# Second norm in plain channel order with five row buffers, square sums first, one sigmoid, and modulation blocks in pairs

## The reference, cut to what matters

```python
sh1, sc1, g1, sh2, sc2, g2 = split(silu(c) @ w_ada + b_ada)      # modulation, 6 x 1024 per row of c
h  = rmsnorm(x, norm1_g) * (1 + sc1) + sh1
q, k, v, u, gate_b, gate_c = split(h @ w_in)
x  = x + g1 * (concat(attention(q, k, v), short_conv(u, ...)) @ w_o)
h2 = rmsnorm(x, norm2_g) * (1 + sc2) + sh2                       # the second norm
scores = sigmoid(h2 @ w_router)                                  # 64 experts, top 8 of 4 groups
routed = sum over 8 chosen experts of gate * (silu(h2 @ w_gate_e) * (h2 @ w_up_e)) @ w_down_e
x  = x + g2 * (routed + shared_expert(h2))
```

## Time and profile before

| | |
|---|---|
| median of 3 runs | 1159.12 us (1158.35 to 1160.63) |
| profiled execution | 1158.43 us, span 1156.4 us |
| PE busy | 1055.1 us (91% of the span) |
| DVE / ACT / POOL busy | 431.3 / 198.2 / 183.5 us |
| mean granted TensorE clock | 0.966 of 2.4 GHz |
| DMA | 372.10 MB, 322 GB/s over the span |
| stages (us from the start) | projection to 263, attention to 370, output projection to 430, second norm and router to 457, routing to 499, expert loop to about 1090, tail |

### The profile page before, as it was taken

One profiled execution on the slowest core, in us unless ns is written; L12 is line 12 of the kernel. 1 busy time (PEld: TensorE's weight loads), 2 busy tenths in 40 slices (PEclk: granted clock), 3 DMA queues, 4 the chain that ended last, 5 costly groups with the idle time before them and its releaser, 6 DMA issues.

```text
span 1156.4 us, 15518 instructions
## 1 busy us (share of the span) xinstructions
PE 1055.1 (91%) x5570; PEld 531.4 (46%) x5570; DVE 431.3 (37%) x933; ACT 198.2 (17%) x427; POOL 183.5 (16%) x240
## 2 busy tenths in 40 slices
PE   5999899998999986889998889988899898999885
PEld 3355455676777566643342323433334333334332
DVE  0445876415554357622322212222122212222156
ACT  4311110003333013001111111111111111111100
POOL 1002223102302001321211111111011211111100
PEclk9999999998999998999998989999999988999998
DMA  9879789964663922599999999999999999999496
GB/s 306 305 276 348 255 311 322 279 218 181 219 171 117 365 78 91 215 406 359 419 404 421 378 377 417 410 408 415 381 408 410 407 355 422 387 417 380 180 411 240
DMA packets 81055, 372.10 MB, mean 322 GB/s; under 512 B 12513, under 2 KB 27438, under 8 KB 52807
## 3 DMA queue, kind: packets, MB, share of 16 engines
q1 hardware_dynamic: 50160, 269.80, 59.3%
q0 software_dynamic: 23312, 69.67, 17.4%
q10 hardware_dynamic: 7540, 32.07, 7.8%
HBM read 354.24 MB, written 58.01 MB: 356 GB/s over the span
## 4 chain that ended last, share of the span: by engine, by line
PE 73%; DMA 14%; DVE 6%; SPq 3%; issue 2%; ACT 1%; POOL 0%; DVEq 0%; ACTq 0%; POOLq 0%
PE pb L1537 23%; DMA mem<-in_w_up_e 11%; PE pb L1555 11%; PE pb L1246 11%; PE pb L1134 5%; PE pb L1401 4%; SPq L717 2%; PE pb L1161 2%; PE pb L1379 2%; PE pb L1252 2%; PE pb L1250 2%; DMA mem<-own_d 2%; PE pb L1333 1%; PE pb L1320 1%; DVE mem L1851 1%
## 5 line engine op out<-in xcount | busy, mean ns | idle before, releaser
L1537 PE MATMUL pb<-mem 128*32 128x512 f32 (+2 forms) x1600 | 332.6, 620 | 39.8 <-DMA mem<-in_w_up_e 36.8
L1537 PEld LDWEIGHTS pb<-mem 128*32 128x32 f32 (+2 forms) x1600 | 106.0, 135 | 218.7 <-issue 214.9
L1555 PE MATMUL pb<-mem 128*32 128x512 f32 (+2 forms) x800 | 159.9, 596 | 2.8 <-ACT mem L1108 2.8
L2060 DVE SCALAR_TENSOR_TENSOR mem<-pb,mem 128x256 f32<-128x256 f32 x44 | 29.9, 679 | 281.0 <-ACT mem L1104 281.0
L1246 PE MATMUL pb<-mem 128*128 128x384 f32 x384 | 130.3, 494 | 2.0 <-DVE mem L1720 2.0
L1134 PE MATMUL pb<-mem 128*128 128x128 f32 (+3 forms) x593 | 89.8, 283 | 29.5 <-DVE mem L1628 10.2
L1134 PEld LDWEIGHTS pb<-mem 128*128 128x128 f32 (+3 forms) x593 | 66.2, 145 | 108.4 <-issue 80.3
L850 POOL DMA_INDIRECT own_d<-mem x44 | 46.3, 1053 | 384.8 <-DVE mem L2067 265.2
L1246 PEld LDWEIGHTS pb<-mem 128*128 128x128 f32 x384 | 71.8, 192 | 62.9 <-issue 10.0
L1555 PEld LDWEIGHTS pb<-mem 128*32 128x32 f32 (+2 forms) x800 | 50.5, 130 | 80.6 <-issue 80.6
L2067 DVE COPY mem<-pb 128x512 f32<-128x512 f32 x44 | 30.4, 692 | 130.3 <-PE pb L1555 130.3
(11 more groups left out here) (268 smaller groups left out, 1024.6 us busy)
## 6 DMA issues: line engine op xcount, KB each, us to landing
mem<-in_w_gate_e SPq DMA_DIRECT2D x64, 1024.0 KB, 11.1
mem<-in_w_up_e SPq DMA_DIRECT2D x64, 1024.0 KB, 14.9
mem<-in_w_down_e SPq DMA_DIRECT2D x64, 1024.0 KB, 14.1
mem<-in_w_ada SPq DMA_DIRECT2D x24, 1024.0 KB, 10.6
mem<-own_d SPq DMA_DIRECT2D x32, 512.0 KB, 15.5
mem<-in_w_in SPq DMA_DIRECT2D x8, 1536.0 KB, 13.5
mem<-new_d POOLq DMA_DIRECT2D x16, 512.0 KB, 7.9
out<-in_cache_k_w ACTq DMA_DIRECT2D x8, 1020.0 KB, 7.8
```

What stands on the lines that cost most here:

```text
L1537: mm = eng.matmul(pb[t % 2][lo:hi, :].rearrange("p (q f) -> p q f", q=2), lhsT=xT[:, k, lo:hi], rhs=wgu[SERVED.index(c) % WB_N][:, :, k, : ...
L1555: mm = eng.matmul(pb[2 + half][lo:hi, :], lhsT=he[:, f, lo:hi], rhs=wdn[SERVED.index(c) % WB_N][:, f, 512 * half:512 * half + 512], start= ...
```

## The change

The h2 rows are now written in plain channel order, so DVE reads and writes adjacent elements, and the step of eight moves into PE's transposes: `every(row, k)` picks the columns k, k + 8, k + 16, ... as the stationary operand. That holds for the five tiles of the second norm and for `x_turn`, since the gathered rows are in plain order too. There are five h2 row buffers in place of two. DVE's order is new: the norms of j = 0, 1, 2 follow pieces u = 11, 12, 13, the four clearing operations move up behind u = 5, and only two norms stand behind the last piece. ACT does four square sums ahead of the first copy-out; one sigmoid serves the four prompt tiles and one the sample tile, with a sigmoid of one element ahead of them. The router's results lie side by side in bank 4, the sample's in bank 5. The two modulation blocks of a chunk stand together behind j = 3 (j = 1 in chunks 6 and 7).

```diff
@@ -421,7 +421,7 @@
         snm, szs, srz = (small[:, 60 + i:61 + i] for i in range(3))
-        h2_row = [at(m_att + D * i, D) for i in range(2)]
+        h2_row = [at(m, D) for m in (m_att, m_att + D, m_mod, m_mod + D, m_mod + 2 * D)]
         sg = at(m_cv, 2, NTOK)
         wd = at(m_hT, 2, D)
         shared_t = [at(m_vr + 512 * i, 512) for i in range(2)]
@@ -569,7 +569,7 @@
         def ada_after(c):
-            return (1, 3) if c < 6 else (0, 1)
+            return 3 if c < 6 else 1
         def tok(j):
             return slice(P * j, P * j + (NS if j == SAMPLE else P))
@@ -579,11 +579,10 @@
-        def chunked(row):
-            return row.rearrange("p (k q) -> p k q", k=KD)
-        def strided(row):
-            return row.rearrange("p (q k) -> p k q", k=KD)
+        def every(row, k):
+            return row.rearrange("p (q k) -> p k q", k=KD)[:, k, :]
         def sc_row(n):
@@ -640,7 +639,7 @@
             for j, tt in enumerate(ORDER):
                 eng.wait_ge(s_h2, j + 1)
-                eng.dma_start(h2_d[tok(tt), 0:D], h2_row[j % 2][0:nt(tt), :]).then_inc(s_h2w[j % 2], 16)
+                eng.dma_start(h2_d[tok(tt), 0:D], h2_row[j][0:nt(tt), :]).then_inc(s_h2w[j % 2], 16)
             eng.wait_ge(s_G, 1)
             eng.wait_ge(s_j, 10)
             eng.dma_start(h2_d[0:SEQ, D:HROW].rearrange("(k p) n -> p k n", p=P), r_gd[:, 0:SAMPLE, :]).then_inc(s_gw, 16)
@@ -1056,7 +1055,8 @@
             for copy in copies[copied + len(COPY_STEPS):]:
                 eng.dma_start(*copy).then_inc(s_caches, 16)
-            for j, tt in enumerate(ORDER):
+            def square(j):
+                tt = ORDER[j]
                 eng.wait_ge(s_x1, 10 + j + 1)
                 if j:
                     eng.wait_ge(s_ss2, j)
@@ -1064,23 +1064,27 @@
                                accum_out=ss2[0:nt(tt), tt:tt + 1]).then_inc(s_ss2, 1)
                 eng.wait_ge(s_var2, j + 1)
                 eng.activation(rs2[0:nt(tt), tt:tt + 1], ss2[0:nt(tt), tt:tt + 1], ACT.Sqrt).then_inc(s_sd2, 1)
-            eng.wait_ge(s_rz, 1)
-            def sigmoid(j):
+            def h2_evac(j):
                 tt = ORDER[j]
-                eng.wait_ge(s_lg, j + 1)
-                eng.activation(r_sc[0:nt(tt), NE * tt:NE * (tt + 1)], pb[4 + j % 2][0:nt(tt), 0:NE], ACT.Sigmoid
-                               ).then_inc(s_sc, 1)
-            for j, tt in enumerate(ORDER):
                 n = nt(tt)
                 for half in range(2):
                     eng.wait_ge(s_h2p, 2 * j + half + 1)
                     eng.activation(h2T[:, 4 * half:4 * half + 4, tok(tt)],
                                    pb[2 + half][:, 0:4 * n].rearrange("p (k n) -> p k n", k=4),
                                    ACT.Copy).then_inc(s_h2T, 1)
-                if j:
-                    sigmoid(j - 1)
-            sigmoid(TILES - 1)
+            for j in range(4):
+                square(j)
+            h2_evac(0)
+            square(4)
+            h2_evac(1)
+            eng.activation(small[0:1, 72:73], cst[0:1, 0:1], ACT.Sigmoid)
+            for j in range(2, TILES):
+                h2_evac(j)
+            eng.wait_ge(s_rz, 1)
+            eng.wait_ge(s_lg, TILES)
+            eng.activation(r_sc[:, 0:NE * SAMPLE], pb[4][:, 0:NE * SAMPLE], ACT.Sigmoid).then_inc(s_sc, 1)
+            eng.activation(r_sc[0:NS, NE * SAMPLE:], pb[5][0:NS, 0:NE], ACT.Sigmoid).then_inc(s_sc, 1)
             for f in range(2):
                 if f:
                     eng.wait_ge(s_route, 2)
@@ -1258,8 +1262,9 @@
                             qk_turn(turned)
                     if z == 29:
                         eng.wait_ge(s_qk, 20)
-                    if j in ada_after(c):
-                        ada(KD + 2 * c + ada_after(c).index(j))
+                    if j == ada_after(c):
+                        for i in range(2):
+                            ada(KD + 2 * c + i)
             for h in (0, 2, 1, 3):
                 for g in range(G):
@@ -1407,10 +1412,9 @@
             def router(j):
                 tt = ORDER[j]
                 eng.wait_ge(s_h2T, 2 * j + 2)
-                if j >= 2:
-                    eng.wait_ge(s_sc, j - 1)
+                to = pb[5][0:NS, 0:NE] if tt == SAMPLE else pb[4][:, NE * tt:NE * (tt + 1)]
                 for k in range(KD):
-                    mm = eng.matmul(pb[4 + j % 2][0:nt(tt), 0:NE], lhsT=h2T[:, k, tok(tt)], rhs=wr[:, k, :],
+                    mm = eng.matmul(to, lhsT=h2T[:, k, tok(tt)], rhs=wr[:, k, :],
                                     start=(k == 0), stop=(k == KD - 1))
                 mm.then_inc(s_lg, 1)
             for j, tt in enumerate(ORDER):
@@ -1419,7 +1423,7 @@
                 for k in range(KD):
                     if k % 4 == 0 and j:
                         eng.wait_ge(s_h2T, 2 * j - 1 + k // 4)
-                    mm = turn(pb[2 + k // 4][:, n * (k % 4):n * (k % 4 + 1)], h2_row[j % 2][0:n, P * k:P * (k + 1)], n)
+                    mm = turn(pb[2 + k // 4][:, n * (k % 4):n * (k % 4 + 1)], every(h2_row[j][0:n, :], k), n)
                     if k % 4 == 3:
                         mm.then_inc(s_h2p, 1)
                 if j:
@@ -1435,7 +1439,7 @@
             def ranks():
-                eng.wait_ge(s_sc, TILES)
+                eng.wait_ge(s_sc, 2)
                 eng.wait_ge(s_M, 2)
                 for j in range(TILES):
                     eng.matmul(pb[7][0:NE, 0:NE], lhsT=onesb[:, 0:NE], rhs=r_mb[:, NE * j:NE * (j + 1)],
@@ -1518,7 +1522,7 @@
             def x_turn(b, landed_):
                 eng.wait_ge(s_ga[b], landed_)
                 for k in range(KD):
-                    mm = turn(pb[4 + k // 4][:, P * (k % 4):P * (k % 4 + 1)], xg[b][:, P * k:P * (k + 1)], P)
+                    mm = turn(pb[4 + k // 4][:, P * (k % 4):P * (k % 4 + 1)], every(xg[b][:, 0:D], k), P)
                     if k % 4 == 3:
                         mm.then_inc(s_tp, 1)
             x_turn(0, 16)
@@ -1843,14 +1847,10 @@
                 tt = ORDER[j]
                 n, s = nt(tt), int(tt == SAMPLE)
-                if j >= 2:
-                    eng.wait_ge(s_h2p, 2 * j - 2)
-                    eng.wait_ge(s_h2w[j % 2], 16 * (j // 2))
-                row = chunked(h2_row[j % 2][0:n, :])
-                link(eng.scalar_tensor_tensor(out=row, in0=strided(x_t[0:n, tt, :]), scalar=rs2[0:n, tt:tt + 1],
-                                              in1=strided(m2[s][1][0:n, :]), op0=ALU.mult, op1=ALU.mult))
-                eng.tensor_tensor(row, row, strided(m2[s][2][0:n, :]), ALU.add).then_inc(s_h2, 1)
+                row = h2_row[j][0:n, :]
+                link(eng.scalar_tensor_tensor(out=row, in0=x_t[0:n, tt, :], scalar=rs2[0:n, tt:tt + 1],
+                                              in1=m2[s][1][0:n, :], op0=ALU.mult, op1=ALU.mult))
+                eng.tensor_tensor(row, row, m2[s][2][0:n, :], ALU.add).then_inc(s_h2, 1)
             eng.wait_ge(s_g1, 16 * (T + 1))
@@ -1867,22 +1867,24 @@
                     eng.wait_ge(s_wg, u + 1)
                     eng.tensor_tensor(x_t[0:n, tt, c0:c0 + w], x_t[0:n, tt, c0:c0 + w], wt[u % 2][0:n, 0:w], ALU.add
                                       ).then_inc(s_x1, 1)
-                    if u in (12, 13):
-                        inverse_rms(u - 12)
-                        second_norm(u - 12)
-            eng.wait_ge(s_vout, 16 * (DIL * G + 1))
-            link(eng.memset(r_mb, 0.0))
-            eng.tensor_copy(onesb, const("ones"))
-            link(eng.scalar_tensor_tensor(out=upperb, in0=const("ident"), scalar=-FAR, in1=const("upper"), op0=ALU.mult,
-                                          op1=ALU.add))
-            eng.memset(r_sc, 0.0).then_inc(s_rz, 1)
-            for j in range(2, TILES):
-                inverse_rms(j)
-            for j in range(2, TILES):
-                second_norm(j)
+                    if u == TILES:
+                        eng.wait_ge(s_vout, 16 * (DIL * G + 1))
+                        link(eng.memset(r_mb, 0.0))
+                        eng.tensor_copy(onesb, const("ones"))
+                        link(eng.scalar_tensor_tensor(out=upperb, in0=const("ident"), scalar=-FAR, in1=const("upper"),
+                                                      op0=ALU.mult, op1=ALU.add))
+                        eng.memset(r_sc, 0.0).then_inc(s_rz, 1)
+                    if 11 <= u <= 13:
+                        inverse_rms(u - 11)
+                        second_norm(u - 11)
+                    if u == 13:
+                        inverse_rms(3)
+            second_norm(3)
+            inverse_rms(4)
+            second_norm(4)
             link(eng.tensor_copy(slotb[:, 0:15], const("slot")[:, 0:15]))
-            eng.wait_ge(s_sc, TILES)
+            eng.wait_ge(s_sc, 2)
             def r3(v):
                 return v.rearrange("p (k n) -> p k n", k=TILES)
```

## The result

The changed kernel takes 1146.32 us (median of 5 runs, 1145.23 to 1150.15) against 1158.75 us of the kernel before, measured beside it (5 runs, 1154.81 to 1160.63). The ratio is 0.991, 95% interval 0.9895 to 0.9925: about 1% faster, where 1177 us and a range from 1149 to 1188 had been forecast. Measured once more later, it was 0.9935 [0.9917, 0.9953]. The profiled execution took 1150.15 us with a span of 1147.9, 8.5 less than the 1156.4 before. It is the slowest of the five, so the profile accounts for 8.5 of the 12.4 us between the medians; the rest lies in the scatter between executions.

A forecast was written before the change was run, and what follows sets the result against it. PE and the DMA engines were taken as nearly full in the expert loop, its waits mostly PE's own work; norm-stage time also counted. -5.5 - 1.0 + 24.7 = +18.2 on 1158.4 gave 1176.6, as median 1177 us, range 1149 to 1188.

The forecast's parts named there:

- the price of a stepped load: PE's transposes: stationary columns in steps of eight cost 1.67 ns each, 213 ns a load, +0.85 us a turn.
- the first rival: PE's transposes: the slower load stays hidden under the pace of the identity's matmul; 1150 us, faster; chance 0.24.
- How many turns count: Expert loop: 29 of the 45 turns on PE lie on the path, at 0.85 us each +24.7 us.
- The second rival: Expert loop: DMA is the real bound and PE's 36.8 us of idle soak up the added work; 1153 to 1159; chance 0.09.
- The norm stage: Second norm and router: adjacent DVE access and the new order end it 5.5 us sooner, 8.0 with turns of 1.03.
- The walk on DVE: Second norm: DVE's new order timed norm by norm, from 424.3 to 439.0, with DVE done 13 us sooner.
- Modulation pairs: Projection phase: paired blocks save one change of pattern in each of eight chunks; -1.0 us, bounds 0 and -2.
- The rival that the new order does not pay: Second norm: ACT's copy-outs wait for the roots; 1182 us with the forecast's load price; chance 0.60 together with the forecast.

The follow-up runs named there:

- the series: Changed kernel with series of transposes and plain float32 matmuls, columns 1, 2, 4 or 8 elements apart, ahead of PE's work; one run, 1216.83 us.

## Why the prediction was wrong

**The step that failed: the price of a stepped load.** The sum took 1.67 ns a column, a load of 213 ns and +0.85 us a turn. The changed kernel shows +0.06. The rate came from L1295, and the series show that it holds there: a plain float32 load with stepped columns runs at 235 / 128 = 1.8 ns a column, and with 32 columns four apart, as at L1295, at 59 / 32 = 1.8. What was wrong was to carry it over to transposes. The profile of before had already told them apart (143 against 192 ns), and the prediction even said so; but it turned the difference into 16 bytes per 1.8 ns for any load, where the whole price should have been scaled. Half of L1295's rate is 0.9 ns a column, 115 ns a load: the very point from which the first rival was said to decide. That rival's mechanism was right in its outcome, though its number was not: it had the penalty as 33 ns for the whole load (92 ns), and the load went from 64 to 117. So it was right with a wrong size, and narrowly: the 117 stands at the edge of its own condition, about 115 ns.

The other error is in the reading of the earlier trace rows. The mean ns of a load there (143, 192) holds more than its share of the pace; it rose by 38 ns while a turn rose by 0.06 / 8, or 8 ns a transpose. What a load costs is to be taken from the pace of a series, start to start.

The Trainium skill, "TensorE: Matmul & The Clock Gate" (LDWEIGHTS, loading the stationary operand), gives the load as the columns over 1.2 GHz, for 128 columns an estimate of 107 ns, and has no term for how far apart they stand; the plain loads with adjacent columns (110 ns) agree, the stepped ones (233 to 240) and the adjacent transposed ones (64) do not. "SBUF — State Buffer" (Door 1: The DMA port swizzle, the note on cachelines) has the price begin where fewer than two reads fall in a line of 16 bytes. The direction agrees; the place does not, since a step of two elements, two reads to a line, costs as much as a step of eight (117 ns each).

**How many turns count: 29 of 45. Too many as well.** Every turn twice put 40.5 us on PE, and 13 to 17 came through, so 15 to 19 turns. The chain of waits showed for before which turns lay beside a load piece; it did not show that PE's waits would shrink by about half of what was added (38.9 to 18.3 us), nor that PE's other work would get some 6 us shorter. The second rival named the first of these, and it is real: with the price of 0.85 us PE's 45 x 0.85 = 38 us would, by the same proportion, have counted for 12 to 16 and not for 24.7, and the sum, its other terms kept, would have been 1165 to 1169, still slower. So this error alone did not turn the sign, the price did.

**The norm stage: -5.5 (-8.0 with turns of 1.03).** Right in its parts, and 3.9 too small in the sum: 2.5 of that is the price of the stepped turns again. The walk on DVE, less the 0.52 of the later mark: rows ready at 424.3, 428.2, 432.1, 435.9 and 439.0, forecast 424.3, 428.2, 432.1, 436.0, 439.0. The first prompt turn starts at 433.39 - 0.52 = 432.9, forecast 433.0; the second at 436.9, forecast 437.4. The last product ends at 447.4 - 0.5, forecast 448.3, and routing starts 9.4 us sooner. The -8.0 was 1.4 too small, 0.5 of it at the second turn and 0.9 from the third copy-out on. That ACT's order ends the stage was right and is now shown: moving only the copy-outs wins 3.1 us there. The forecast counted on a high clock here, and in the profiled run it did not stay high: PE had the first prompt turn at 0.56 and the product behind it at 0.59. It cost nothing, since in the repeated run of the changed kernel both ran at 1.00 and the second turn still waited for the second copy-out, with the routing 31.5 us behind the mark both times:
```profile
437.83 1.14 PE L1138 MATMUL pb<-mem 128*128 128x128 f32 x8 [1.91 <-ACT mem L1073]
```
The whole is more than the sum of the two edits: rows alone -5.8, order alone -1.5, both -9.4 us. It fits that faster norms also serve sooner the roots that hold up the copy-outs, which DVE served at 436.1 with the old rows (mark 415.42) and at 432.6 with the plain ones (mark 416.58); no run separates this from the buffers.

**Modulation pairs: -1.0.** The projections are 1.1 us shorter in the changed kernel's profile and 0.8 with the pairs alone, and the total can't tell it. Two blocks take 1.85 where two single ones took 2 x 0.99.

**The rival that the new order does not pay.** With the old rows it was right for the total (1.0006), with the plain rows wrong. It named the cause, copy-outs behind roots.

**The chances.** Faster had 0.29, slower 0.66. The rival of a hidden load had 0.24 and gave 1150; the result is 1146. The rows bounded the load between 92 and 270 ns, and the value was taken in the upper part of that; with a decision point of 115 inside the bounds and one uncertain carry-over, the chances should have stood nearer to even.

## What to carry to other kernels

Before a price per element is carried from one kind of instruction to another, scale it by what the two cost with the same plain access; and take a load's cost from the pace of a series, since what fits beside the other pass does not lengthen the pace. Where an engine has idle time for data in a loop, double the disputed work before counting additions at full price: here 58 to 68% of it vanished. And where an engine's list mixes producers for others with its own waits, put the copy-out that another engine waits for ahead of the wait.
